# Rebuilding the first norm around whole input tiles, and moving the weight buffers by 64 bytes

## The reference, cut to what matters

```python
# c, c_ctx: (1024,); mod_w[l]: (1024, 6144)
sh1, sc1, g1, sh2, sc2, g2 = split(silu(c) @ mod_w[l] + mod_b[l], 6)      # and the same of c_ctx
h  = rmsnorm(x,  norm1_w[l]) * (1 + sc1) + sh1                            # 512 latent tokens
hc = rmsnorm(cx, norm1_w[l]) * (1 + csc1) + csh1                          # 256 context tokens
...                                                                       # h @ w_in[l], mixers, merge
x  = x + g1 * y
h2 = rmsnorm(x, norm2_w[l]) * (1 + sc2) + sh2
x  = x + g2 * conv_ffn(h2, ...)
```

## Time and profile before

| | |
|---|---|
| median of 3 runs | 3284.24 us (3282.95 to 3288.33) |
| the profiled execution: its time, its span | 3285.47 us, 3283.7 us |
| busy: TensorE, weight loads, VectorE, ScalarE, GpSimd | 92%, 81%, 37%, 29%, 34% of the span |
| mean granted TensorE clock | 0.960 |
| first product of the first mixer | 69.4 us after the start |
| read from HBM, mean rate | 236 MB, 75 GB/s |

### The profile page before, as it was taken

The page is one execution under the profiler, slowest core; times in us unless marked ns, Lnnn a source line. Parts: engine busy times, 40 slices in busy tenths (PEclk is TensorE's granted clock), DMA queues, the critical chain, the costliest instruction groups (busy, mean ns, idle before and its releaser), DMA issues. The chain is left out here.

```text
span 3283.7 us, 47734 instructions
## 1 busy us (share of the span) xinstructions
PE 3007.3 (92%) x19520; PEld 2662.5 (81%) x19520; DVE 1220.4 (37%) x2793; ACT 956.8 (29%) x1600; POOL 1128.8 (34%) x614
## 2 busy tenths in 40 slices
PE   5888999999999997999999769889999999889996
PEld 3788897798888996888888658787888879878885
DVE  2444415524332014332333544532532330254455
ACT  2222314433223112222222132222533322232332
POOL 2122330053335323333333232332143335354453
PEclk9999999999999998999999879899999999989998
DMA  5012120012222115111211211212022232322222
GB/s 195 27 52 73 38 91 14 7 59 99 78 78 74 68 52 205 62 58 61 76 57 61 88 67 52 78 44 79 20 81 91 91 115 78 116 78 103 90 94 93
DMA packets 39670, 249.78 MB, mean 76 GB/s; under 512 B 4512, under 2 KB 4896, under 8 KB 14112
## 3 DMA queue, kind: packets, MB, share of 16 engines
q1 hardware_dynamic: 36576, 236.25, 20.3%
q10 hardware_dynamic: 2880, 10.49, 0.8%
HBM read 236.23 MB, written 10.49 MB: 75 GB/s over the span
## 5 line engine op out<-in xcount | busy, mean ns | idle before, releaser
L1872 POOL TENSOR_TENSOR w_rest<-raw,w_head 128x2048 fp32r<-128x2048 f32 (+2 forms) x172 | 740.7, 4307 | 1101.3 <-ACT w_head L1043 1072.2
L688 PE MATMUL psum_products<-w_head,h_head 128*128 128x256 f32 x2368 | 692.6, 293 | 0.0
L688 PE MATMUL psum_products<-w_rest,h_head 128*128 128x256 f32 x2368 | 679.3, 287 | 0.0
L688 PE MATMUL psum_products<-w_head,h_rest 128*128 128x256 f32 x2368 | 678.7, 287 | 0.0
L688 PE MATMUL psum_products<-h_head,w_head 128*128 128x512 f32 (+3 forms) x1696 | 602.6, 355 | 18.4 <-POOL h_rest L1898 16.3
L688 PE MATMUL psum_products<-h_head,w_rest 128*128 128x512 f32 (+3 forms) x1696 | 601.0, 354 | 0.0
L688 PE MATMUL psum_products<-h_rest,w_head 128*128 128x512 f32 (+3 forms) x1696 | 599.7, 354 | 0.0
L688 PEld LDWEIGHTS psum_products<-w_head,h_head 128*128 128x128 f32 x2368 | 464.1, 196 | 2.6 <-issue 1.3
L688 PEld LDWEIGHTS psum_products<-w_rest,h_head 128*128 128x128 f32 x2368 | 464.1, 196 | 0.5
L688 PEld LDWEIGHTS psum_products<-w_head,h_rest 128*128 128x128 f32 x2368 | 463.5, 196 | 0.0
L1043 ACT ACTIVATE w_head<-raw 128x2048 fp32r<-128x2048 f32 (+2 forms) x172 | 307.7, 1789 | 478.0 <-PE psum_products L688 437.9
(11 more groups left out here) (237 smaller groups left out, 4036.0 us busy)
## 6 DMA issues: line engine op xcount, KB each, us to landing
raw<-in_stream SPq DMA_DIRECT2D x198, 1024.0 KB, 4.8
raw<-in_stream SPq DMA_DIRECT2D x20, 512.0 KB, 3.2
residual<-stage ACTq DMA_DIRECT2D x16, 512.0 KB, 3.0
stage<-residual SPq DMA_DIRECT2D x14, 512.0 KB, 4.8
stage<-in_x SPq DMA_DIRECT2D x8, 512.0 KB, 5.2
stage<-in_ctx SPq DMA_DIRECT2D x4, 512.0 KB, 8.2
out<-stage ACTq DMA_DIRECT2D x4, 512.0 KB, 2.6
rope_r<-in_rope_r SPq DMA_DIRECT2D x2, 768.0 KB, 4.3
```

Of the source, the lines that this page charges most:

```text
L688: return nc.tensor.matmul(o, a, b, start=start, stop=stop)
L1872: G.tensor_tensor(wl[:, s["sp"] % 2, 0:n], raw[:, s["n"] % 2, 0:n], wh[:, s["sp"] % 2, 0:n].bitcast(F32), ALU.subtract).then_inc(*ev.mark( ...
```

## The change

**The first norm.** All of x and ctx is loaded into `x_in` (laid over `h_rest`) before any modulation slot. The eight slots needed first have a buffer each, `mods_a` and `mods_b`, laid over parts of the arena that are not yet in use, so their loads wait for nothing. Seven steps "enter" take the tiles through square sum, power, scale, turn and a VectorE copy to `x_turned` (laid over `acc`), without modulation. From the fourth on each is followed by a pair of vectors, a scale slot and its shift slot. Four steps "affine_k" then apply the affine step in place, from SBUF to SBUF, to two k-tiles each, with ScalarE's copy and GpSimd's subtraction per k-tile of 768 tokens. The two early splits stand between them. The gates' first bank waits for each k-tile (`by_k`) and not for tiles.

**The places.** 64 bytes are allocated ahead of `w_head` and 64 behind `w_rest`, and the arena is 128 bytes shorter; `w_head` and `w_rest` now begin 64 bytes past a multiple of 128, and all other buffers stand at multiples as before.

```diff
@@ make_plan
+    FIRST = [4, 0, 5, 1, 6, 2, 7, 3]
@@
-            first = dict(count=TILES + 2, l=0, use="first", tiles=list(range(TILES)), gen=gen)
-            ticks("norms", stop=1, **first)
-            for _ in vectors(2 * D // COLS):
-                pass
-            step("affine", l=0, which=0)
-            ticks("norms", start=1, **first)
+            mods, early = [], []
+            for i, n in enumerate(FIRST):
+                mods.append(cols("mod_w", 0, n * COLS, splits=False, home=i))
+                if i == 1:
+                    early.append(slot(0, ("w_in", 0, [(IN_OFF["mg"], 16)])))
+                if i == 3:
+                    early.append(slot(0, ("w_in", 0, [(IN_OFF["mq"], P), (IN_OFF["mk"], P)])))
+            turns = []
+            for k in range(TILES + 1):
+                step("enter", k=k)
+                if k >= 3:
+                    turns += [vector(0, FIRST[2 * (k - 3) + i], mods[2 * (k - 3) + i]) for i in range(2)]
+                    for turn in turns[-2:]:
+                        step("vector", **turn)
+            for j in range(3):
+                step("affine_k", j=j)
+                if j < 2:
+                    plan.append(dict(kind="split", slot=early[j]))
+            step("affine_k", j=3)
@@ buffers
+        xin = nc.alloc_sbuf_tensor_at("x_in", [P, TILES, D], F32, offset=H_REST)
+        xT = nc.alloc_sbuf_tensor_at("x_turned", [P, KD, TOK], F32, offset=ACC)
         raw = sb("raw", [P, 2, SLOT])
+        sb("half_line", [P, 16])
         wh = sb("w_head", [P, 2, SLOT], F32R)
         wl = sb("w_rest", [P, 2, SLOT], F32R)
+        sb("other_half", [P, 16])
@@ SP
-            load(0)
-            load(1)
-            loaded = 2
             sp.dma_start(par[:], ins["params"]).then_inc(*ev.mark("par_in", "par", by=16))
-            sp.dma_start(const[:], ins["consts"]).then_inc(*ev.mark("const_in", "const", by=16))
+            loaded = 10
+            for i in range(loaded):
+                load(i)
@@ ScalarE
+                elif kind == "affine_k":
+                    for k in (2 * st["j"], 2 * st["j"] + 1):
+                        act.wait_ge(*ev.at("hf_k", k))
+                        nc.scalar.activation(hh[:, k, :], xT[:, k, :], ACT.Copy).then_inc(*ev.mark("act", "hh_k", k))
@@ VectorE
+                elif kind == "enter":
+                    k = st["k"] - 1
+                    if 0 <= k < TILES:
+                        dve.wait_ge(*ev.at("x_turn", k))
+                        for half in range(2):
+                            V.tensor_copy(xT[:, 4 * half:4 * half + 4, k * P:(k + 1) * P],
+                                          psm[:, 2 * (k % 2) + half, :].rearrange("p (k c) -> p k c", k=4)).then_inc(
+                                *ev.mark("dve", "x_turned", k))
+                elif kind == "affine_k":
...
+                    for k in (2 * st["j"], 2 * st["j"] + 1):
+                        for q, t0, size in seqs[True]:
+                            V.tensor_scalar(xT[:, k, t0:t0 + size], xT[:, k, t0:t0 + size], aff[:, 0, 0, k, q:q + 1],
+                                            vec[:, 0, k, q:q + 1], ALU.mult, ALU.add).then_inc(
+                                *ev.mark("dve", "hf_k", k))
@@ GpSimd
+                elif kind == "affine_k":
+                    for k in (2 * st["j"], 2 * st["j"] + 1):
+                        pool.wait_ge(*ev.at("hh_k", k))
+                        G.tensor_tensor(hl[:, k, :], xT[:, k, :], hh[:, k, :].bitcast(F32), ALU.subtract).then_inc(
+                            *ev.mark("pool", "h_k", k))
```

More of the change, by code:

```diff
@@ L113, in make_plan, with slot @@
 def make_plan():
-    plan, stream, bank, split = [], [], [0], [0]
-    def slot(l, blocks, kt=KD, splits=True):
-        s = dict(n=len(stream), l=l, blocks=blocks, kt=kt, cols=sum(b[1] for b in blocks[2]), sp=None)
+    plan, stream, bank, split, ring = [], [], [0], [0], []
+    def slot(l, blocks, kt=KD, splits=True, home=None):
+        s = dict(n=len(stream), l=l, blocks=blocks, kt=kt, cols=sum(b[1] for b in blocks[2]), sp=None, home=home)
+        if home is None:
+            s["r"] = len(ring)
+            s["before"] = ring[-2]["n"] if len(ring) >= 2 else None
+            ring.append(s)
         if splits:
@@ L144, in pairs, with cols, vector @@
         return (0, 1, 2) if ctx else (1, 2)
-    def cols(name, l, c0, n=COLS, kt=KD, row=0, splits=True):
-        return slot(l, (name, row, [(c0, n)]), kt, splits)
-    modulation = iter([(l, n) for l in range(DEPTH) for n in range(6 * D // COLS)])
+    def cols(name, l, c0, n=COLS, kt=KD, row=0, splits=True, home=None):
+        return slot(l, (name, row, [(c0, n)]), kt, splits, home)
+    FIRST = [4, 0, 5, 1, 6, 2, 7, 3]
+    modulation = iter([(l, n) for l in range(DEPTH) for n in range(6 * D // COLS) if l or n >= len(FIRST)])
+    made = [0]
+    def vector(l, n, s):
+        turn = dict(slot=s, l=l, n=n, g=made[0], piece=1)
+        made[0] += 1
+        step("vector", s, l=l, n=n, g=turn["g"], piece=0)
+        return turn
     def vectors(count):
@@ L305, in make_plan @@
     for st in plan:
[L306 to L309, removed]
+        if st["kind"] == "split":
+            order.append(st)
+            done += 1
+            continue
         if st["slot"] is not None:
@@ L313, in make_plan @@
             if sp is not None and not st.get("open") and sp + 1 < len(splits):
-                waiting = [s["n"] for s in stream[n:splits[sp + 1]["n"]] if s["sp"] is None and s["n"] not in used]
+                waiting = [s["n"] for s in stream[n:splits[sp + 1]["n"]]
+                           if s["sp"] is None and s["home"] is None and s["n"] not in used]
                 upto += len(waiting) <= 1
@@ L336, in annotate @@
         st["i"] = i
-        own_banks = kind == "arot" and not st["first"] or st.get("ticks", range(1)).start > 0
+        own_banks = kind == "arot" and not st["first"] or st.get("ticks", range(1)).start > 0 or st.get("k", 0) > 0
         st["prev"] = None if own_banks else last.get("mixing")
@@ L807, in _ @@
                         ha = [lambda k, x=x: x[:, k, t0:t0 + size] for x in (hh, hl)]
-                        three(psg[0:16, n % RING, 0:size], wa, ha, range(KD), True).then_inc(
+                        three(psg[0:16, n % RING, 0:size], wa, ha, range(KD), True,
+                              by_k=not st["gen"] and n == st["bank"]).then_inc(
                             *ev.mark("pe", "bank", n))
@@ L1054, in _ @@
                         if k < n:
[L1056 removed]
+                            act.wait_ge(*ev.at("rsum", st["gen"], k))
                             if k >= 2 and use != "last":
```

106 lines of the change are left out of this document (82 added, 24 removed).

## The result

The changed kernel takes 3265.46 us (median of 5 runs, 3261.97 to 3273.58) against 3284.24 (5 runs); the ratio is 0.9947, 95% interval 0.9931 to 0.9964. So it is faster, by 18.8 us between the medians, where I had forecast 3.5. The profiled execution took 3262.7 us (span 3260.9, mean clock 0.958).

What follows compares the result with a forecast made beforehand. TensorE, busy 3007 of 3284 us, was taken as the bound, with a start where it waits. The start's gates' products would end at 76.6 instead of 80.13, the 64 bytes give nothing: 3284.2 - 3.5 = 3281 us, range 3220 to 3292.

Steps and rivals of the forecast that it cites:

- the first rival: The places of w_head and w_rest matter to TensorE's products: 3115 to 3270 us; 27%, plus 3% beyond the range.
- my own case: The start gains 3.5 us and the 64 bytes nothing: 3281 us; 3276 to 3284 has 46%.
- wrong as a whole if that spacing moves by even 1 ns: Sign against the prediction: the spacing of warm 256-column products on TensorE, 0.120 us before, changes.
- Arrival and tiles: At the start, parameters arrive at 14.5 us, ScalarE starts at 14.6, tiles are scaled by 33.7, vector pairs start at 26.1.
- The clock: TensorE reaches 2.4 GHz during the first or second pair; vectors end at 43.8 us, or 54.7 at the lower level throughout.
- the slow rival: TensorE stays at the lower clock level until the vectors are done, at 54.7 us; 3292 us in all; 10%.
- GpSimd's work: Behind the vectors, GpSimd's eight subtractions and the two splits between them take 19.7 us.
- The hold of VectorE: In the affine step, VectorE's SBUF-to-SBUF operations wait for GpSimd's: 2.8 us, bounds 0 and 5.
- The gates' second bank: Its 24 products start at the lower clock level, eleven at 0.43 us, the rest at 0.23: 7.7 us, ending at 76.6.
- The 64 bytes: Moving w_head and w_rest changes nothing in TensorE's 15,432 products: taken as 0, bounds 0 and 170 us.

Runs made afterwards that it cites:

- e6_act_affine: The changed kernel with the affine step of each k-tile on ScalarE instead of VectorE's four TENSOR_SCALARs; 3260.48 us, ratio 0.9939 to the kernel before.
- e2_norm: The changed kernel without the 64 bytes, so the rebuilt first norm alone; 3277.7 us, ratio 0.9981 to the kernel before.
- p2_probe: Products alone at the kernel before's addresses, weight buffers moved by 0 to 4160 bytes; h over 512 columns 227, 233, 229 ns at 0, 64, 192.
- e4_all: The kernel before with 64 bytes ahead of the first buffer, h_head, so all operands move together; 3282.1 us, ratio 0.9997.
- p3_probe: Products alone at the kernel before's addresses, both w buffers stepped through places with 0 in between; 256-column forms 113.3 and 117.8 ns at 64 and 192.
- p1_probe: Products alone in the kernel's four forms, at pairs of places of weight and other buffers; w over h 117.6 ns at (0,0), (32,32), (64,64).
- e5_splits_first: The changed kernel with both early splits ahead of the four affine steps; 3260.26 us, ratio 0.9926 to the kernel before.

## Why the prediction was right, and in which step it was not

The direction was right and 3265 lies in the range, but through the first rival and not through my own case; that it lies there is owed to the width of the range and not to the sum. By the sign that I named, "wrong as a whole if that spacing moves by even 1 ns", my case was wrong: w over h went from 119.8 to 117.3. And the rival had its size wrong: it put 3 or 4 ns per product first, which on my sum is 3219 to 3235 and not 3225 to 3240; the measured mean is 14.9 us over 15,336 products, 1 ns. Step by step:

- **Arrival and tiles.** Right: ScalarE starts at 14.54 (14.6), the pairs at 26.11 (26.1).
- **The clock.** Right: the level rose during the first pair, as one of the two cases foresaw, and the slow rival is out. The vectors end at 43.1 (43.8).
- **GpSimd's work.** 20.15 us (19.7), beginning at 45.04 (45.7).
- **The hold of VectorE.** The mechanism is right, shown by `e6_act_affine`, where it is gone with VectorE's operations; the size was 1.9 us and not 2.8 (2.1 by GpSimd's stretch in that run). The Trainium skill ("Advanced Engine Details and Errata", VectorE Performance Modes) says that the two interfere; 1.65 against 4.75 and 10.32 us for the same four operations agree.
- **The gates' second bank.** Mis-sized: six products at the lower level and not eleven, 0.9 us less. GpSimd's end at 66.96 and not 68.2, by the terms above, gives another 1.2, so the copy came at 74.5 and not at 76.6, and the start gave 5.6 us where I had 3.5; `e2_norm` alone gives 5.8, interval 3 to 9.
- **The 64 bytes.** This step failed: "I take nothing", where they are worth 15.3 us (interval 14 to 22). The bound was there, 0 to 170, and I chose its end by two arguments. The first, that fp32 pairs at the same places show no excess, carried a finding from one kind of matmul to another; that was no evidence on products in fp32r. The second, that the excess is "alike for 256 and 512 columns, as a fixed cost would be", was accidental: with the distance it goes from 13 to 11 or 7 ns for 256 columns (120, 118, 113.3 less 106.7) and from 14 to 20 ns for 512 (227, 233 less 213.3). The rows could not give its size, nor that one form loses what three gain; they did say that the excess was unexplained, and the first rival's odds were the honest answer to that.

The Trainium skill ("SBUF — State Buffer", Who interferes with whom) makes the port pair of VectorE and GpSimd the only contention of engines. The probes agree in this: the paces move with TensorE alone at work, so the places act within it. The Trainium skill ("TensorE: Matmul & The Clock Gate", Back-to-back issue gap) gives N / 2.4 + 2.5 ns, here 109 and 216, for an isolated product and not for a stream with a weight load to each product, as these are; my comparison passed over that. No place met it: the best paces are 113.3 and 226.7.

What stays open: why the distance counts inside TensorE, and what picks one of the two paces.

## What to carry to other kernels

Where an engine is busy for nine tenths and its instructions take longer than their columns, measure that excess by itself before anything else: a small program of the kernel's own products at its own addresses, with the distance between operands as the only variable, needs one run of under a millisecond. Here it pointed to 192 bytes, which in the kernel are worth twice what the change won. A single number for "the pace" hides forms that go opposite ways. Moving a buffer for any reason can move the time by some tenths of a per cent either way (64 bytes: -15.3 us, 128: +12.5, 192: -37), so an edit that shifts allocations is to be compared against one that only shifts them.

## What the runs showed of the hardware

- The pace of back-to-back fp32r products depends on the distance of their operands' addresses in a partition with a period of 256 bytes (as far as 4096), not on the addresses (`p2_probe`; `e4_all`, where all operands moved together, keeps every pace): 113.3 to 121.7 ns for 256 columns, 226.7 to 235.5 for 512.
- At 64 and 192 bytes there are two steady paces for 256 columns, 113.3 and 117.8 ns (`p3_probe`), at times kept through a whole step of 55 us and its forms, at times changed between two forms; at 0 there is one, 120. At one arrangement of `p1_probe` h over 512 also has two, 228.9 and 232.9.
- VectorE's four TENSOR_SCALARs from SBUF to SBUF, 1.65 us alone, take 4.75 beside GpSimd's subtractions (`e5_splits_first`), while GpSimd gets two operations through and then pauses for 1.24.
